# A modulation product moved from TensorE to VectorE, in a kernel of two transformer blocks

## The reference, cut to what matters

```python
c_act = jax.nn.silu(c)                       # c: (1, 1024)
mod = c_act @ ada_w[l] + ada_b[l]            # (1, 1024) @ (1024, 6144)
shift1, scale1, gate1, shift2, scale2, gate2 = split(mod, 6)
h = rmsnorm(x, norm1_g[l]) * (1.0 + scale1) + shift1
proj = h @ w_in[l]                           # forgetting + stick-breaking attention follow
x = x + gate1 * (merged @ w_out[l])
h2 = rmsnorm(x, norm2_g[l]) * (1.0 + scale2) + shift2
y = hierarchical_moe(h2, ...)                # 16 experts, top 2 of the best group of 4
x = x + gate2 * y
```

## Time and profile before

| | us |
|---|---|
| median of 3 runs (724.62 to 724.89) | 724.63 |
| span of the profiled execution | 723.3 |
| TensorE busy | 697.1 |
| VectorE busy | 397.3 |
| ScalarE busy | 328.3 |

### The profile page before, as it was taken

How to read it: one execution, slowest core, us unless ns; L and a number is a source line. 1 busy time by engine, 2 the same in 40 slices (tenths; PEclk the granted TensorE clock), 3 DMA queues, 4 the chain that set the end, 5 groups by cost and what they waited for, 6 DMA issues and landing times.

```text
span 723.3 us, 10224 instructions
## 1 busy us (share of the span) xinstructions
PE 697.1 (96%) x4002; PEld 481.2 (67%) x4002; DVE 397.3 (55%) x722; ACT 328.3 (45%) x540; POOL 2.6 (0%) x5
## 2 busy tenths in 40 slices
PE   5999999999999999999999999998999999999894
PEld 3999989767777776799977777674344343344342
DVE  5654734776856978644665576856233333323325
ACT  6543434654758466444457776433123223213214
POOL 1000000000000000000000000000000000000000
PEclk9999999999999999999999999999999999999998
DMA  8974666753645449766334435879999999999961
GB/s 353 420 287 178 220 251 250 288 228 132 233 135 215 171 179 363 295 264 242 117 133 170 162 118 196 325 294 421 397 429 416 433 426 430 420 427 429 418 259 58
DMA packets 20011, 202.18 MB, mean 280 GB/s; under 512 B 2434, under 2 KB 3458, under 8 KB 7428
## 3 DMA queue, kind: packets, MB, share of 16 engines
q1 hardware_dynamic: 19248, 200.61, 69.8%
q10 hardware_dynamic: 724, 1.05, 0.4%
HBM read 200.59 MB, written 1.05 MB: 279 GB/s over the span
## 4 chain that ended last, share of the span: by engine, by line
PE 53%; DMA 3%; DVE 2%; ACT 2%; issue 1%; ACTq 0%; DVEq 0%
PE psum L1248 13%; PE psum L1296 7%; PE psum L892 7%; PE psum L893 7%; PE psum L894 7%; DMA ring<-in_expert_w_down 3%; PE psum L1211 3%; PE psum L1191 2%; PE psum L1132 1%; PE psum L998 1%; PE psum L1147 1%; DVE ring_rounded L1829 0%; PE psum L1273 0%; ACT ring_rounded L1485 0%; PE psum L1129 0%
## 5 line engine op out<-in xcount | busy, mean ns | idle before, releaser
L1829 DVE TENSOR_TENSOR ring_rounded<-ring,ring_rounded 128x1024 fp32r<-128x1024 f32 (+1 forms) x131 | 153.8, 1213 | 60.8 <-ACT ring_rounded L1485 60.7
L1485 ACT ACTIVATE ring_rounded<-ring 128x1024 fp32r<-128x1024 f32 (+1 forms) x132 | 129.7, 1037 | 6.6 <-PE psum L894 6.6
L892 PE MATMUL psum<-hT_rounded,ring_rounded 128*128 128x256 f32 x360 | 102.8, 286 | 0.0
L893 PE MATMUL psum<-work_rounded,ring_rounded 128*128 128x256 f32 x360 | 101.8, 283 | 0.0
L894 PE MATMUL psum<-hT_rounded,ring_rounded 128*128 128x256 f32 x360 | 101.8, 283 | 0.0
L893 PE MATMUL psum<-ring_rounded,hT_rounded 128*128 128x512 f32 (+1 forms) x224 | 86.5, 386 | 0.0
L1248 PE MATMUL psum<-ring,work 128*64 128x512 f32 x320 | 83.8, 592 | 1.3 <-issue 1.3
L892 PE MATMUL psum<-ring_rounded,hT_rounded 128*128 128x512 f32 (+1 forms) x208 | 83.1, 400 | 0.0
L894 PE MATMUL psum<-ring_rounded,work_rounded 128*128 128x512 f32 (+1 forms) x208 | 80.0, 384 | 0.0
L892 PEld LDWEIGHTS psum<-hT_rounded,ring_rounded 128*128 128x128 f32 x360 | 69.0, 192 | 3.0 <-issue 2.5
L893 PEld LDWEIGHTS psum<-work_rounded,ring_rounded 128*128 128x128 f32 x360 | 69.0, 192 | 0.1
(11 more groups left out here) (296 smaller groups left out, 1056.8 us busy)
## 6 DMA issues: line engine op xcount, KB each, us to landing
ring<-in_chunks SPq DMA_DIRECT2D x44, 2048.0 KB, 8.4
ring<-in_expert_w_down SPq DMA_DIRECT2D x16, 2048.0 KB, 16.1
ring<-in_expert_w_gate SPq DMA_DIRECT2D x12, 2048.0 KB, 15.4
ring<-in_expert_w_up SPq DMA_DIRECT2D x8, 2048.0 KB, 18.4
gates<-in_expert_w_up SPq DMA_DIRECT2D x8, 1024.0 KB, 21.3
hT<-in_expert_w_gate SPq DMA_DIRECT2D x4, 1024.0 KB, 16.0
mixed<-in_expert_w_gate SPq DMA_DIRECT2D x4, 1024.0 KB, 18.1
ring<-in_chunks SPq DMA_DIRECT2D x4, 512.0 KB, 7.7
```

Source lines behind the costliest of these rows:

```text
L892: nc.tensor.matmul(out, a[0], b[0], start=start, stop=False, skip_group_check=True)
L893: nc.tensor.matmul(out, a[0], b[1], start=False, stop=False, skip_group_check=True)
L1485: nc.scalar.activation(as_rounded(high_piece(c, q)), src[:, piece_of(c, q)], ACT.Copy).then_inc(chunk_hi, 1)
L1829: v.tensor_tensor(as_rounded(w[:, piece]), w[:, piece], was_rounded(high_piece(c, q)), ALU.subtract)\
```

## The change

A tile of 128 output features by 1024 inputs of `ada_w`, transposed on the host, is multiplied on VectorE by silu(c) broadcast to all partitions and summed along the row in the same instruction; the sum lands in its column of `mod`. Each chunk has 4 such tiles, 48 in all, and each is a step ("ada", c, j) of VectorE alone. silu(c) is made from `c_rows` (512 KB, loaded before the fourth chunk) by a sigmoid on ScalarE and a product on VectorE after "cz"; it lives in `gate_rows` until the gates need the place. The bias is added to the columns. For the gates, ("mod", c) units turn columns of `mod` into rows: four fp32 matmuls by the identity, with the column broadcast as weights, and VectorE copies the bank into `gate_rows`. The steps are placed anew, and an ada slot of the ring comes free by `ada_done`.

```diff
+    ada = [(c, j) for c in range(2 * N_MOD) for j in range(ADA_TILES)]
+    def some_ada(n=1):
+        for _ in range(n):
+            steps.append(("ada",) + ada.pop(0))
...
     for name in ("cz", "bz", "az", "ax", "cq", "ck"):
         unit("fm", name, 0)
+        if name == "cz":
+            steps.append(("c_rows",))
         if name == "ck":
             unit("mix", 0)
+        some_ada(dict(bz=1, az=1, ax=1, cq=1, ck=1).get(name, 0))
         unit("fm", name, 1)
-        if name in ("ax", "ck"):
-            some_ada()
+        some_ada(dict(cz=1, bz=1, az=1, cq=2, ck=2).get(name, 0))
...
-        if u in (("tm", "g4", 0), ("tm", "g5", 1), ("tm", "g3", 1)):
-            some_ada()
+        if u in (("fm", "bq", 0), ("fm", "bq", 1), ("bkv",), ("tm", "g4", 1), ("tm", "g5", 1), ("tm", "g2", 1), ("tm", "g3", 1)):
+            some_ada(2 if u == ("fm", "bq", 0) else 1)
...
     for u in (("tm", "va", 1), ("tm", "vb", 1), ("fm", "qa", 0), ("fm", "qa", 1),
               ("fm", "ka", 0), ("fm", "ka", 1)):
         unit(*u)
-        if u == ("fm", "qa", 1):
-            some_ada()
-    some_ada(mod_only=True)
+        some_ada(2 if u[0] == "fm" else 1)
+    steps.append(("gate_cols", 0))
     unit("fa",)
     steps.append(("logf",))
     unit("fm", "qb", 0)
+    some_ada(2)
     unit("FT",)
+    unit("mod", 4)
+    unit("mod", 5)
...
     for u, n in seq:
         unit_and_heads(u, n)
+        some_ada(min(len(ada), 2 if u[0] == "fm" else 1))
...
-    steps += [("sigmoid", 8), ("mods", 1)]
+    steps += [("sigmoid", 8), ("mods", 1), ("gate_cols", 1)]
     unit("proj", "s", 0, 0)
+    unit("mod", 10)
+    unit("mod", 11)
...
-                if last_use:
-                    sp.wait_ge(unit_done, last_use)
+                if held:
+                    wait_chunk_used(sp, held)
...
+                    pe.wait_ge(gate_cols_ready, 1 if c < N_MOD else 2)
+                    for j in range(ADA_TILES):
+                        last = nc.tensor.matmul(b[:, j * P:(j + 1) * P], mod[:, c, j:j + 1].to_broadcast([P, P]), ident,
+                                                start=True, stop=True)
-                elif kind == "ada":
-
-                    w = wait_chunk(pe, u).rearrange("p (k n) -> p k n", n=W512)
-                    if u[1] == 0:
-                        pe.wait_ge(c_ready, 1)
-                    for k in range(KD):
-                        j = k % 4
-                        at = 32 * k + GATHERED - 1 - ada_row(u[1])
-                        last = nc.tensor.matmul(b[32 * j:32 * j + 32, :], c_wide[:, at:at + 32], w[:, k, :],
-                                                start=k < 4, stop=k >= 4, skip_group_check=True)
...
+            def c_rows_silu():
+
+                dve.wait_ge(c_sigmoid_ready, 1)
+                link(v.tensor_tensor(c_rows, c_rows, c_sigmoid, ALU.mult))
+
+            def ada(c, j):
+
+                tile = wait_chunk(dve, ("ada", c))[:, j * D:(j + 1) * D]
+                v.scalar_tensor_tensor(tile, tile, 1.0, c_rows, ALU.mult, ALU.mult, accum_out=mod[:, c, j:j + 1]).then_inc(ada_done, 1)
+
+            def add_ada_b(first, n):
+
+                dve.wait_ge(ada_done, ADA_ORDER.index((first + n - 1, ADA_TILES - 1)) + 1)
+                bias = vec[:, VEC["ada_b"]][:, 4 * first:4 * (first + n)].rearrange("p (c j) -> p c j", j=4)
+                return v.tensor_tensor(mod[:, first:first + n, :], mod[:, first:first + n, :], bias, ALU.add)
+
+            def gate_cols(i):
+
+                add_ada_b(GATE_CHUNKS[2 * i], 2).then_inc(gate_cols_ready, 1)
...
-                        last = v.tensor_tensor(row, b[:, :], row, ALU.add)
...
+                    last = v.tensor_copy(gate_rows[:, c // N_MOD, (c % 2) * W512:(c % 2 + 1) * W512], b[:, :])
...
+        return np.ascontiguousarray(w.T.reshape(ADA_TILES, P, D).transpose(1, 0, 2).reshape(P, -1))
```

More of the change, by code:

```diff
@@ L57 @@
 ADA_EARLY = 8
-GATHERED = 4
+ADA_TILES = 4
+GATE_CHUNKS = (4, 5, 10, 11)
 LEFT = 640
@@ L323, in plan @@
     unit("rank")
[L324 to L328, removed]
+    steps += [("slots",), ("weigh",)]
+    assert not ada
     split = []
@@ L381, in chunk_of @@
 def chunk_of(step):
-    if step[0] == "unit" and step[1] == "ada":
-        return [("ada", step[2])]
+    if step[0] == "ada":
+        return [step[:2]]
     if step[0] == "split":
@@ L400 @@
 SILU = ("cz", "bz", "az")
[L401 to L407, removed]
+ADA_ORDER = [s[1:] for s in STEPS if s[0] == "ada"]
 def evictor(u):
-    if u[0] == "ada" and ada_row(u[1]):
-        return "dve"
-    if u[0] in ("tm", "bkv", "fa", "FT", "ada") or (u[0] == "fm" and u[1] not in SILU) or (u[0] == "xT" and u[2] == 0):
+    if u[0] in ("tm", "bkv", "fa", "FT") or (u[0] == "fm" and u[1] not in SILU) or (u[0] == "xT" and u[2] == 0):
         return "act"
@@ L425, in last_reader @@
 def last_reader(chunk, first=False):
+    if chunk[0] == "ada":
+        at = max(i for i, s in enumerate(STEPS) if chunk in chunk_of(s))
+        return sum(s[0] == "unit" for s in STEPS[:at]) + 1
     n = [i for i, u in enumerate(UNITS) if chunk in chunk_of(("unit",) + u)][0 if first else -1]
@@ L433, in place_chunks @@
 def place_chunks():
-    free, uses, slots, loads = [0] * RING, [0] * RING, [], []
+    free, uses, slots, loads, held = [0] * RING, [0] * RING, [], [], [None] * RING
     for c in CHUNKS:
         s = min(range(RING), key=lambda s: free[s])
-        slots.append((s, free[s]))
+        slots.append((s, held[s]))
+        held[s] = c
         uses[s] += c != FIRST
@@ L441, in place_chunks @@
         free[s] = last_reader(c)
-    return slots, loads, uses, sorted((at, s) for s, at in enumerate(free))
+    return slots, loads, uses, sorted((at, s, held[s]) for s, at in enumerate(free))
 SLOTS_OF_CHUNKS, LOADS_OF_SLOT, DENSE_LOADS, SLOTS_LEFT = place_chunks()
@@ L692, in wait_chunk, with wait_chunk_used @@
             return slot(c)
+        def wait_chunk_used(eng, c):
+            if c[0] == "ada":
+                eng.wait_ge(ada_done, ADA_ORDER.index((c[1], ADA_TILES - 1)) + 1)
+            else:
+                eng.wait_ge(unit_done, last_reader(c))
         def slot(c):
@@ L1177, in _ @@
                     begun = True
-                elif s[0] == "unit" and s[1:] != LAST_MOD:
+                elif s[0] == "unit":
                     unit(n, s[1:], (1,) if begun else (0, 1))
@@ L1402, in unit @@
                     last = nc.scalar.activation(dst, b, ACT.Copy)
[L1403 to L1407, removed]
                 elif kind == "bkv":
@@ L1740, in unit @@
                     c = u[1]
-                    if c // 2 in (2, 5):
-                        dve.wait_ge(gate_rows_loaded, 16)
-                        row = gate_rows[:, c // 2 == 5, (c % 2) * W512:(c % 2 + 1) * W512]
-                        last = v.tensor_tensor(row, b[:, :], row, ALU.add)
-                    else:
-                        first = c - GATHERED + 1
-                        bias = vec[:, VEC["ada_b"]][:, 4 * first:4 * (c + 1)].rearrange("p (c j) -> p c j", j=4)
-                        last = v.tensor_tensor(mod[:, first:c + 1, :], b[:, 0:4 * GATHERED].rearrange("p (j c) -> p c j", j=4),
-                                               bias, ALU.add)
-                elif kind == "ada":
-                    dve.wait_ge(*evicted(("ada", u[1] - 1)))
-                    last = v.tensor_tensor(ada_acc[:, :], b, ada_acc[:, :], ALU.add)
+                    last = v.tensor_copy(gate_rows[:, c // N_MOD, (c % 2) * W512:(c % 2 + 1) * W512], b[:, :])
                 elif kind == "proj":
```

83 lines of the change are left out of this document (28 added, 55 removed).

## The result

| | us | ratio to before, 95% interval |
|---|---|---|
| before, 4 runs beside it | 724.76 (724.62 to 724.97) | |
| changed kernel, 4 runs | 717.74 (716.75 to 720.32) | 0.9907 [0.9894, 0.9919] |
| changed kernel again, 5 runs on another occasion | 719.58 (718.84 to 719.96) | 0.9926 [0.9912, 0.9939] |

The change makes the kernel faster, by 7.0 us and by 5.4 us on the second occasion, under 1% both times. I had forecast 12.2 us. The profiled execution is the longest of the first four (720.32 us, span 718.5, 4.8 less than before).

What follows compares the result with a forecast made beforehand. TensorE was taken to bound the kernel to about 500 us, then TensorE and weight loads together; 18.6 - 3.6 - 4.8 + 2.0 = 12.2 us gained, giving 712.4 us. Range 705 to 725, likeliest 709 to 716 (chance 0.50).

Steps and rivals of the forecast that it cites:

- rival 2: Twice the forecast VectorE lateness plus 2 us of waits for ring chunks: 719 us (716 to 721), chance 0.13.
- between units that are ready on both sides: Seven ada units and two gathering mods there: removal gains their full length, 7 x 1.85 + 2 x 0.79 = 14.5 us.
- new mod units: Four added TensorE units, after the forget gate and in the second block's projections: 0.9 us each, 3.6 us back.
- third rival: VectorE becomes the bound at 2.3 us a tile: 734 us; chance 0.15 together with anything slower.
- VectorE's lateness at the end of the second attention: Tiles delay VectorE 2.4 us at pairs 14 and 15, another 2.4 before projection s: 4.8 us lost.
- mod 4 and ada 5: Before the first transposes of "merged": removing these 2.7 us of TensorE work gains 1.3 us.
- mod 5 and ada 6: Covering the second norm of tile 0: removing these 2.7 us of TensorE work gains 0.9 us.
- ada 7: Covering the second norm of tile 1, where transposes already waited 0.64 us: removal gains 0.
- ada 10: At the last transposes of "merged", where VectorE is late anyhow: removal gains 0.7 us.
- pair-14 wait: Second attention: VectorE's subtraction for pair 14 comes late, a delay shared by pair 15: 2.4 us lost.
- the term of the experts: Experts start with fewer bytes due, so most of their 2.2 us of down-weight waits goes: 2.0 us gained.
- ada 11 and mod 11: At the making of the one-hot and the first gathers: removing both together gains 0.3 us.

Runs made afterwards that it cites:

- e3: The changed kernel with every VectorE tile done twice: 743.18 us, ratio 1.0265.
- e1: The changed kernel with eleven groups of unused identity multiplications filling TensorE's idle places: 715.21 us, ratio 0.986.
- e2: The changed kernel with each VectorE tile cut to 16 of its 1024 columns (values wrong): 711.28 us, ratio 0.982.
- e5: The changed kernel with four of the 48 tiles moved from the second attention to units g0 and g1: 713.51 us, ratio 0.9833.
- e6: e5 plus fills of TensorE's idles as in e1, but none at pair 14 and one group ahead of rank instead of the gathers: 711.18 us, ratio 0.9809.
- e10: The changed kernel unchanged, run again beside the kernel before: 719.58 us, ratio 0.9926.
- e7: e6 with the four spread-row units moved to TensorE's idle places, their copies on ScalarE and fewer fills: 710.19 us, ratio 0.9794.
- e4: The kernel before with three ada units cut from 16 TensorE multiplies of 512 columns to 4 of 32 (values wrong): 724.96 us, ratio 1.0001.
- e8: The kernel before with e4's cuts and spread rows 4 and 5 cut to 32 columns (values wrong): 728.27 us, ratio 1.0048.

## Why the prediction was right and where it was wrong

**Right.** The sign, the wide range, and that TensorE's work is what counts up to rank. My likeliest band, 709 to 716, was missed: 717.7 lies in the band of rival 2, and neither of its reasons came true, twice my lateness or waits for the ring. So the wide range held for a reason that stands nowhere in it. Where a unit stood between units that are ready on both sides it was worth its length: 2.03 us for each ada unit by the unit ends (I took 1.85, which leaves out the gap to its neighbour). The new mod units cost 0.91 each; 4 and 5 had 0.7 more behind them, most of it the wait for L1388 (0.5 us, last row of the waits above), which I had not seen. The tile was cheaper than I took it, 1.14 us of VectorE's time instead of 1.3. The Trainium skill's rule of half rate ("Vector Engine (DVE) Microarchitecture Reference", section 7) doesn't hold here: 1.217 us for two fp32 SBUF sources with the sum kept, against 1.213 for the product without one. My third rival hung on that price; e3 shows the rival's mechanism to be real. VectorE's lateness at the end of the second attention was forecast at 2.4 + 2.4 us and measured, with the clock up, at 3.0 + 1.8 (e1), and e2 shows it to be the tiles'. Where the four last tiles stand decides much of it: e5 moved them, and 1.8 + 0 were left (e6's column). Neither TensorE nor VectorE waited for a chunk of the ring.

**A sign of being wrong that came.** I had written that I am wrong if TensorE's waits before the experts sum to over 15 us. From 8 us, behind the wait for the norm row, to the gathers they sum to 18.5 us in the changed kernel, 6.5 in the kernel before. The sign was badly set: by my own steps 11 us of idle come in (1.4, 1.8, 1.9 and 1.2 at the lost covers, 4.8 of lateness) on top of these 6.5. I had that idle in the sum as work not gained and didn't ask what it does to the work behind it.

**Wrong: the steps "mod 4 and ada 5", "mod 5 and ada 6", "ada 7" and "ada 10".** I took the worst case of a lost cover to be a gain of nothing. They were negative in the profiled run, -0.8, -0.9, about -1 and -0.3, because the idle that takes the cover's place lets the granted clock fall, and the work behind it runs at 1.2 GHz. With the idles filled, the same four gave +0.8, +0.7, 0 and +1.4: the original terms within 0.7 us. The pair-14 wait is the same story, 4.5 instead of 3.0. Up to rank the columns "changed" and "e1" differ by 6.7 us; without the falls my 9.9 stands against 10.4, closer than the single terms, which are off by up to 0.7 us either way and partly cancel. The profile before held the clue and I passed it by: 1.00 in every stretch, and no idle over 1.1 us from 12 us, behind TensorE's first waits, to 460 us.

**Wrong: the term of the experts.** I expected the waits for down weights to shrink by 2.0; they went from 2.2 to 2.0 us. From rank on the gain was 1.0 us (1.2 in e6), where I had 0.3 + 2.0. In e6 and in the changed kernel alike the first gate products end 14.3 to 14.5 us after rank instead of 15.3, and from there on the distances stay the same: I put the gain down to ada 11 and mod 11. In e2, e5 and the profiled run of e10, with a slow stretch from 2 to 2.5 us behind rank on, only 0.3 us of it are left. Fewer bytes ahead of the two loads did not shorten the waits for them; I did not test what holds them.

**In sum.** 12.2 forecast, 7.0 measured at the median, between runs with clocks of 0.991 and 0.988 against 0.996 before, which stands for two to four falls: some 2 to 3 us at the average price. The tail gave 1.3 less, the wait at FT took 0.7. In the profiled run, with six falls, the forecast missed by 7.4.

## What to carry to other kernels

Work that TensorE does in somebody else's shadow isn't free to remove: ask how long it will idle there, and count 0.8 us on average, up to 1.6, for each fall of the clock behind a new idle of some 2 us; not every such idle brings one. Useful units (here the four spread rows) do better in such places than between busy neighbours, though of the 3.6 us hoped for only 1.0 was left at the end (e7 against e6). And VectorE is full long before its busy share says so where it takes turns with ScalarE (late at 77 of 96 us here, not late at 57 of 60 elsewhere): put extra tiles where it waits for nobody. The fastest kernel here, e7, is 2% under the kernel before, while the change as made gave 1%.

## What the hardware did that I had not expected

The granted clock fell at idles of 1.7 to 2.9 us next to transposes or small matmuls, for 3.4 us at a time (6.8 once each in e3 and e10), and not each time: e4 had 1.5, 2.0 and 2.3 us without a fall, and the same 1.91 us idle was followed by a fall in one trace and not in another. Eleven groups of fills (some 10 us of multiplications for nothing, by an estimate from the spread-row units' 0.91 each) brought its mean from 0.982 to 0.991 up to 0.994 to 0.997, and a kernel with 6 us less TensorE work was 3.2 us slower (e8). The read of VectorE's accumulator takes 0.08 us and overlaps: the next VectorE instruction starts with it where it waits for nothing.
